# One number and one branch for each pair of experts, with the even split last in the code

## What is computed

```python
gates = jnp.sum(jax.nn.one_hot(flat_idx, N_EXPERTS, dtype=jnp.float32)
                * (g_w * e_w)[..., None], axis=1)
y = jnp.zeros((b * s, d), jnp.float32)
for e in range(N_EXPERTS):
    hid = jax.nn.silu(xt @ w_gate[e]) * (xt @ w_up[e])
    y = y + gates[:, e:e + 1] * (hid @ w_down[e]).astype(jnp.float32)
```

## Time and profile before

| | |
|---|---|
| median of three runs | 1491.67 us (1491.1 to 1496.73) |
| the profiled execution | 1496.81 us, span 1494.9 us |
| PE busy | 1265.8 us, 85% of the span |
| PEld, DVE, ACT, POOL busy | 755.1, 393.0, 286.0, 73.6 us |
| mean granted clock of TensorE | 0.917 |
| expert stages, first to last L639 | 255 to 521 us and 767 to 1028 us |

### The profile page before, as it was taken

The page is one execution under the profiler, slowest core; times in us unless marked ns, Lnnn a source line. Parts: engine busy times, 40 slices in busy tenths (PEclk is TensorE's granted clock), DMA queues, the critical chain, the costliest instruction groups (busy, mean ns, idle before and its releaser), DMA issues.

```text
span 1494.9 us, 17527 instructions
## 1 busy us (share of the span) xinstructions
PE 1265.8 (85%) x7188; PEld 755.1 (51%) x7191; DVE 393.0 (26%) x1064; ACT 286.0 (19%) x566; POOL 73.6 (5%) x126
## 2 busy tenths in 40 slices
PE   4999986779999869988768999984999877988896
PEld 1756434334444247653434343431877756756672
DVE  0213324111111025821341111112133665312122
ACT  2213311001011021142211010101103444221101
POOL 3000001000000030000000000000001221000000
PEclk9799996989999989998778999997999989998898
DMA  9976960779999969852529999999244423242000
GB/s 343 326 288 251 347 246 3 279 291 394 396 393 393 393 220 339 306 184 99 182 89 330 369 392 393 396 395 338 67 159 127 131 75 126 69 167 67 0 14 28
DMA packets 159080, 351.49 MB, mean 235 GB/s; under 512 B 4853, under 2 KB 7069, under 8 KB 159005
## 3 DMA queue, kind: packets, MB, share of 16 engines
q1 hardware_dynamic: 152776, 340.94, 62.7%
q0 software_dynamic: 4704, 6.50, 1.8%
q10 hardware_dynamic: 1524, 2.95, 0.6%
HBM read 349.25 MB, written 1.12 MB: 234 GB/s over the span
## 4 chain that ended last, share of the span: by engine, by line
PE 79%; DVE 6%; issue 5%; ACT 5%; DMA 3%; SPq 1%; DVEq 0%; ACTq 0%
PE bank L399 24%; PE bank L639 22%; PE bank L409 10%; PE bank L622 4%; PE bank L664 4%; PE bank L431 3%; DMA ring<-in_w_ada 2%; PE bank L443 2%; DMA ring<-in_moe_w_up 1%; PE bank L879 1%; PE bank L452 1%; PE bank L463 1%; ACT arena L939 1%; SPq L321 1%; PE bank L557 1%
## 5 line engine op out<-in xcount | busy, mean ns | idle before, releaser
L639 PE MATMUL bank<-ring,arena 128*32 128x512 f32 x3072 | 342.7, 602 | 40.6 <-issue 31.5
L399 PE MATMUL bank<-arena,ring 128*128 128x256 f32 x1600 | 363.3, 390 | 6.2 <-DVE arena L1295 2.8
L399 PEld LDWEIGHTS bank<-arena,ring 128*128 128x128 f32 x1600 | 313.0, 196 | 58.4 <-issue 5.6
L639 PEld LDWEIGHTS bank<-ring,arena 128*32 128x32 f32 x3072 | 112.2, 111 | 258.9 <-issue 258.9
L409 PE MATMUL bank<-ring,arena 128*128 128x512 f32 x352 | 157.8, 608 | 2.4 <-issue 2.4
L409 PEld LDWEIGHTS bank<-ring,arena 128*128 128x128 f32 x352 | 68.0, 195 | 89.4 <-issue 88.5
L622 PE MATMUL bank<-arena 128*128 128x128 f32 x512 | 70.3, 302 | 20.9 <-issue 20.9
L622 PEld LDWEIGHTS bank<-arena 128*128 128x128 f32 x512 | 67.8, 216 | 33.6 <-issue 32.8
L431 PE MATMUL bank<-ring,c_rep 128*32 128x512 f32 x480 | 68.4, 701 | 12.2 <-DMA ring<-in_w_ada 6.4
L1643 DVE TENSOR_TENSOR arena<-arena,bank 128x512 f32<-128x512 f32 x16 | 11.0, 688 | 228.2 <-PE bank L639 228.2
L980 ACT ACTIVATE arena<-bank 128x512 f32<-128x512 f32 x41 | 24.5, 596 | 238.4 <-PE bank L399 185.2
(11 more groups left out here) (267 smaller groups left out, 980.6 us busy)
## 6 DMA issues: line engine op xcount, KB each, us to landing
ring<-in_moe_w_gate SPq DMA_DIRECT2D x32, 2048.0 KB, 14.3
ring<-in_moe_w_up SPq DMA_DIRECT2D x32, 2048.0 KB, 18.5
ring<-in_moe_w_down SPq DMA_DIRECT2D x32, 2048.0 KB, 12.9
ring<-in_w_ada SPq DMA_DIRECT2D x24, 2048.0 KB, 12.9
ring<-in_w_in SPq DMA_DIRECT2D x16, 2048.0 KB, 9.2
ring<-in_w_c SPq DMA_DIRECT2D x6, 2048.0 KB, 10.0
ring<-in_ev_w_in SPq DMA_DIRECT2D x5, 2048.0 KB, 20.1
ring<-in_od_w_in SPq DMA_DIRECT2D x5, 2048.0 KB, 7.9
```

Of the source, the lines that this page charges most:

```text
L399: mm = pe.matmul(ps[k0][:, t * S:(t + 1) * S], w[:, k, c:c + P], rhs[:, k, :], start=(k == 0), stop=(k == KT - 1))
L639: mm = pe.matmul(bank[col:col + CHUNK, :], lhs[:, k, col:col + CHUNK], ring[:, s0 + e, cut], start=start, stop=stop, tile_position=(0, col))
```

## The change

`split` holds one number a pair instead of three flags. TensorE reads it once and tests it once around the whole work of the pair: `first_pair`, `middle_pair` and `last_pair` each stand three times, for n = 1, 3 and 2 in this order. What was outside the tests (gather, scatter, the turned blocks, the waits) is inside now. VectorE's rule prefers n = 2: 1 only if the first expert has up to 32 tokens and the second over 64, 3 if the first has over 64, else 2. The rows that the experts get follow from it. TensorE's wait for `late_ready` stands behind the last pair. The other lines of `gate_up` and `down` are the same, one level further out.

```diff
-        split = sb("split", [P, LAYERS, CHUNKS - 1, PAIRS], I32)
+        split = sb("split", [P, LAYERS, PAIRS], I32)
...
-                def by_split(splits, emit):
-
-                    for n in range(1, CHUNKS):
-                        with pe.If(splits[n - 1] > 0):
+                def by_split(which, emit):
+
+                    for n in (1, 3, 2):
+                        with pe.If(which == n):
                             emit(n)
...
-                def gate_up(j, splits):
+                def gate_up(j, n):
 
                     pe.wait_ge(sem("x_cur_act"), j + (done + 1))
                     pe.wait_ge(sem("x_cur_dve"), j + (done + 1))
                     if not isinstance(j, int) or j:
                         pe.wait_ge(sem("g_cur_ready"), j + done)
-                    def products(n):
-                        for bank, m0 in ((4, 0), (5, 2)):
...
-                    by_split(splits, products)
+                    for bank, m0 in ((4, 0), (5, 2)):
...
-                def down(j, splits, last=False):
+                def down(j, n, last=False):
...
-                    def products(n):
-                        for half in range(2):
...
-                    by_split(splits, products)
-
-                def splits_of(j):
+                    for half in range(2):
...
+                def split_of(j):
                     col = slice(j, j + 1) if isinstance(j, int) else bass.ds(j, 1)
-                    return [pe.value_load(split[0:1, layer, n, col], min_val=0, max_val=1) for n in range(3)]
+                    return pe.value_load(split[0:1, layer, col], min_val=1, max_val=3)
+
+                def first_pair(n):
+                    gate_up(0, n)
+                    gather(1)
+                    down(0, n)
+
+                def last_pair(n):
+                    gate_up(PAIRS - 1, n)
+                    results(PAIRS - 2)
+                    scatter(PAIRS - 2)
+                    down(PAIRS - 1, n, last=True)
+                    results(PAIRS - 1)
+                    scatter(PAIRS - 1)
 
                 gather(0)
+                by_split(split_of(0), first_pair)
+                with pe.Fori(1, PAIRS - 1) as j:
+
+                    def middle_pair(n):
+                        gate_up(j, n)
+                        results(j - 1)
+                        gather(j + 1)
+                        scatter(j - 1)
+                        down(j, n)
+
+                    by_split(split_of(j), middle_pair)
+                by_split(split_of(PAIRS - 1), last_pair)
                 pe.wait_ge(sem("late_ready"), layer + 1)
-                splits = splits_of(0)
-                gate_up(0, splits)
-                gather(1)
-                down(0, splits)
-                with pe.Fori(1, PAIRS - 1) as j:
-                    splits = splits_of(j)
-                    gate_up(j, splits)
-                    results(j - 1)
-                    gather(j + 1)
-                    scatter(j - 1)
-                    down(j, splits)
...
-                for c in range(2):
-                    step(dve.tensor_scalar(other[:, :, c], number_of[:, :, 0], float(CHUNK * (c + 1)), None, ALU.is_le))
-                step.wait()
-                step(dve.tensor_copy(split[:, layer, 0, :], other[:, :, 0]))
...
+                step(dve.tensor_scalar(few, number_of[:, :, 0], float(CHUNK), None, ALU.is_le))
+                step(dve.tensor_scalar(other_many, number_of[:, :, 1], 2.0 * CHUNK, None, ALU.is_gt))
+                step(dve.tensor_scalar(many, number_of[:, :, 0], 2.0 * CHUNK, None, ALU.is_gt))
+                step.wait()
+                step(dve.tensor_tensor(few, few, other_many, ALU.mult))
+                step.wait()
+                step(dve.tensor_tensor(lean, many, few, ALU.subtract))
+                step.wait()
+                step(dve.tensor_scalar(split[:, layer, :], lean, 2.0, None, ALU.add))
```

More of the change, by code:

```diff
@@ L648, in gate_up @@
                         pe.wait_ge(sem("g_cur_ready"), j + done)
-                    def products(n):
-                        for bank, m0 in ((4, 0), (5, 2)):
[L651 to L656, removed]
-                    by_split(splits, products)
+                    for bank, m0 in ((4, 0), (5, 2)):
+                        landed(m0, j)
+                        landed(m0 + 1, j)
+                        for k in range(KT):
+                            mm = chunks(ps[bank], x_cur, k, m0, slice(k * 512, k * 512 + 512), n,
+                                        k == 0, k == KT - 1)
+                        mm.then_inc(unit_done, 2)
                 def scatter(j):
@@ L722, in experts @@
[L722 to L728, removed]
+                    for half in range(2):
+                        for f in range(4):
+                            mm = chunks(ps[6 + half], hidT, f, 4,
+                                        slice(f * D + half * 512, f * D + half * 512 + 512), n,
+                                        f == 0, f == 3)
+                        if half == 0:
+                            mm.then_inc(sem("down_full"), 1)
+                        else:
+                            mm.then_inc(unit_done, 2)
@@ L1553, in route @@
                 mask_of = rt[:, 512:544].rearrange("p (t j a) -> p t j a", t=TT, a=2)
[L1554 removed]
                 slots = rt[:, 636:652].rearrange("p (j a) -> p j a", a=2)
[L1556 removed]
+                number = rt[:, 652:668]
                 dve.wait_ge(sem("rank_full"), layer + 1)
@@ L1562, in route @@
                 number_of = number.rearrange("p (j a) -> p j a", a=2)
-                for c in range(2):
-                    step(dve.tensor_scalar(other[:, :, c], number_of[:, :, 0], float(CHUNK * (c + 1)), None, ALU.is_le))
+                few, many, other_many, lean = (rt[:, 708 + 8 * n:716 + 8 * n] for n in range(4))
+                step(dve.tensor_scalar(few, number_of[:, :, 0], float(CHUNK), None, ALU.is_le))
+                step(dve.tensor_scalar(other_many, number_of[:, :, 1], 2.0 * CHUNK, None, ALU.is_gt))
+                step(dve.tensor_scalar(many, number_of[:, :, 0], 2.0 * CHUNK, None, ALU.is_gt))
                 step.wait()
-                step(dve.tensor_copy(split[:, layer, 0, :], other[:, :, 0]))
-                step(dve.tensor_tensor(rt[:, 708:716], other[:, :, 1], other[:, :, 0], ALU.subtract))
-                step(dve.tensor_scalar(rt[:, 716:724], other[:, :, 1], -1.0, 1.0, ALU.mult, ALU.add))
-                step(dve.tensor_tensor(n_other, other[:, :, 0], other[:, :, 1], ALU.add))
+                step(dve.tensor_tensor(few, few, other_many, ALU.mult))
                 step.wait()
-                step(dve.tensor_copy(split[:, layer, 1:3, :], rt[:, 708:724].rearrange("p (n j) -> p n j", j=PAIRS)))
+                step(dve.tensor_tensor(lean, many, few, ALU.subtract))
                 step.wait()
-                step(dve.tensor_scalar(slots[:, :, 0], n_other, -float(CHUNK), 3.0 * CHUNK, ALU.mult, ALU.add))
-                step(dve.tensor_scalar(slots[:, :, 1], n_other, float(CHUNK), float(CHUNK), ALU.mult, ALU.add))
+                step(dve.tensor_scalar(split[:, layer, :], lean, 2.0, None, ALU.add))
+                step(dve.tensor_scalar(slots[:, :, 0], lean, float(CHUNK), 2.0 * CHUNK, ALU.mult, ALU.add))
+                step(dve.tensor_scalar(slots[:, :, 1], lean, -float(CHUNK), 2.0 * CHUNK, ALU.mult, ALU.add))
                 step.wait()
```

1 line of the change is left out of this document (removed).

## The result

The changed kernel takes 1505.78 us, median of 4 runs (1505.07 to 1511.62), against 1491.38 us for the kernel before in 4 runs of the same session. The ratio is 1.0101 with a 95% interval of 1.0063 to 1.0139: slower by 1.0%. The forecast was 1494 us in a range of 1480 to 1516, with "same" slightly ahead of "slower". By the prediction's own line of 7.5 us this is "slower", which had 0.38, and not "same", which had 0.45. The time lies in the range, but outside the forecast case's own range of 1484 to 1501: it is inside only because the range was drawn wide enough for rival A's 1512. That much is luck, so the steps need a look. The ratios in this text leave out two runs far above their fellows, one of before (1787.64 us) and one of the kernel with only the new rule (4811.25 us).

A forecast was written before the change was run, and what follows sets the result against it. Weight transfers and TensorE's waits for its own code were taken to bound the expert stages. Layer 0's -6.6 and layer 1's +8.7 us sum to +2.1 on the median of 1491.67: 1494 us, range 1480 to 1516.

The forecast's parts named there:

- forecast case: The prediction's main account, both layers' changes summed to 1494 us; 1484 to 1501 by itself, chance 0.45.
- rival A: Code fetches strictly in turn: a second jump right behind another costs 3.5 us more under load; 1512 us, chance 0.22.
- What bounds the kernel: Expert stages: weight transfers take 31.9 us a pair against TensorE's 30.9, and waits for TensorE's own code.
- The jumps of the new code: Skipped bodies of nearly two blocks: far jumps once per layer, 6.2 us, 7.2 behind another; idle 3.2 and 4.2.
- step (1): Layer 0, first pair: split is read earlier, two idle jumps of 3.2 and 4.2; gate and up start 3.0 us late.
- Step (2): Layer 0, first pair: the 9.20 us gap goes; down starts 19.5 us later and ends at 284.8 against 292.2.
- step (4): Layer 0, second pair: no jump in its body, 4.17 us gone twice; down ends at 326.6 against 334.2.
- step (5): Layer 0 transfers: they run steadily from earlier, so the last "up" weights land 5.5 us earlier, at 492.3.
- Step (6): Layer 0, last pair: first jump hits, second costs 7.2 us; gate starts at 488.6, up at 495.6 against 502.2.
- Layer 1: Second expert stage: four jumps in a row behind the first pair and a lowered clock, +8.7 us in all.
- Rival B: Jumps at the tests are cheap, 3.2 us each with no extra for a second one; 1466 us, chance 0.15.
- Rival C: The loop's eight blocks aren't kept, so each pass pays three jumps of 6.2 us; +175, 1667 us, chance 0.08.

## Why the prediction was near, and what was off

**What bounds the kernel: right.** The passes follow at 31.92 to 31.93 us behind the "up" transfers, against 31.9 worked out from the queue's rate, from the fifth pair of layer 0 on. The 16 us that two reads and some tests fewer were worth did not show; that the reads bring nothing was tested by itself.

**The jumps of the new code: right in place and kind.** Every one of the ten slow tests stands where the count of instructions had put it, and the first test in front of the last pair hits (329 ns). The prices were 3.34 and 4.65 (3.2 and 4.2 forecast), 6.24 and 7.47 (6.2 and 7.2). The gaps: 12.56 for 12.3, 23.92 for 23.3, 6.53 for 6.1.

**Layer 0, steps (1) to (6), -6.6 forecast, +2.0 measured: wrong, and in two terms.** The first is step (1)'s place of the read. The first test began 3.3 us behind the gather's start (246.9 against 243.59), not 1.9; with the dearer idle jumps that makes 2.0 us. The forecast had the first products start 3.0 us later against the gather than before, and they started 5.3 later (11.7 against 6.4), outside the "2 to 4" of its own list of signs. The second and larger is the clock behind a gap. Step (2) and step (4) took 13.94 us for the products of gate and up; they took 15.73 and 15.87. The windows of the changed kernel around them and one undisturbed product between them (length, busy us, PEclk, DMA share, GB/s):

```profile
255.30:271.10 15.80, 15.80 (x129) 0.88 0.34 110
296.00:311.90 15.90, 15.90 (x129) 0.88 0.54 186
327.10:341.00 13.90, 13.90 (x132) 1.00 1.03 394
490.80:506.60 15.80, 15.78 (x129) 0.88 0.95 359
```

A mean of 0.88 says that the products behind the gaps of 7.15, 12.56 and 6.53 us ran partly at 1.2 GHz; it costs them 1.8 to 1.9 us each. The prediction had charged that in one place, layer 1's long gap, and left it out behind the four others that it forecast itself, three of them in layer 0. It gave as its condition a gap of over 20 us, but its own rows show slow products behind shorter ones: the 15.64 of the earlier trace rows stands behind 3.76, and in the earlier trace rows 112 matmuls took 14.85 behind 3.63, where 112 at the full clock take 12.2. With 2.0, 1.8 and 1.9 the steady transfers begin 5.7 us later than step (5) had it, which is all of the 5.5 that it promised: its "up" weights 5.5 us earlier did not come. SyncE's line L356 in the changed kernel, 470 to 476, the answer to the earlier trace rows:

```profile
L356 SPq DMA_DIRECT2D ring<-in_moe_w_up x2: 3103/4133/5163, 468.8 to 472.1; - x2
...
DMA to landing us min/median/max: 17.6/19.2/20.9
```

Issued at 472.1, the last "up" weights land 20.9 later at 493.0, 249.4 us behind the first gather; before it was 497.8 less 248.8, 249.0. Step (6) misses the clock twice: the "up" product of the loop's last pass, behind its wait of 2.43 us, took 8.77 instead of 7.07, and the last pair's gate and up 15.73 again, 3.5 us together. In all 9.2 us, where the layer was off by 8.6.

**Layer 1, +8.7 forecast, +11.0 measured: right, a little small.** From the first product to the last down product 262.8 us were forecast and 265.4 came, 2.6 more. The last pair's gate began 1.2 late (244.7 us behind the first product against 243.5); the pass before it had lost 1.7 to the clock (978.52, 8.77 us instead of 7.07). The same clock behind the last gap is 1.9 more (15.87 instead of 13.94), and the way from there to the down product was 0.5 shorter than forecast.

**What the clock did in the whole kernel** is less than the products' row says. They took 7.3 us more than before (342.7 to 350.0), but the gathers and scatters took less. Their rows, before and after:

```profile
L622 PE MATMUL bank<-arena 128*128 128x128 f32 x512 | 70.3, 302 | 20.9 <-issue 20.9
L664 PE MATMUL bank<-arena 128*128 128x512 f32 x128 | 60.9, 620 | 6.8 <-issue 5.0 <-DVE arena L1651 1.8
...
L622 PE MATMUL bank<-arena 128*128 128x128 f32 x512 | 63.2, 283 | 0.0
L661 PE MATMUL bank<-arena 128*128 128x512 f32 x128 | 57.9, 595 | 1.8 <-DVE arena L1651 1.8
```

The three groups together took 473.9 us before and 471.1 after. Before, the jumps stood between products and gather, and the gather ran slowly behind them (5.13 us); now they stand in front of the products. So the clock isn't a new cost of the change. It is a term that the forecast booked on one side only: step (2) took the gather's gain (3.84 for 5.13) and not what the products would lose. Nor is the length of the gap the whole of it. The products of gate and up took 13.94 us behind 1.51 in the kernel without tests, in the one with the even split first and in layer 1 of the changed kernel. But they were slow behind 2.10 in layer 1 of before:

```profile
837.07 15.64 PE L639 MATMUL bank<-ring,arena 128*32 128x512 f32 x128 [2.10 <-issue]
```

They were slow too behind 1.64, with another gap of 2.2 shortly before it, in the kernel with only the new rule (126 matmuls in 16.78 us) and in the one with the tests around the products (123 in 15.36). No run held the gaps and changed the clock alone, so it isn't shown which gaps bring it down.

**Rival A, fetches strictly in turn: wrong.** A second miss right behind another costs 1.2 to 1.3 us more, not 3.5 (7471 and 7568 ns against 6242 and 6244). Its packets overlap: in layer 0 the two of the second miss began 0.3 us apart (291.14 and 291.46) and took 1.4 and 2.1 us, where the one of the first miss took 1.1. 1512 was nearer to the time than 1494, for another reason than the rival gave.

**Rival B, cheap jumps: wrong under load, right when idle.** 6.2 against 3.3 us for the same kind of jump.

**Rival C, the loop isn't kept: wrong by one block.** It was given 0.08 and 1667 us; one body more brings 1773. (Its sum should give 1654: three jumps of 6.2 less 2.7 are 15.9, not 17.) The prediction said that no run showed the fit, and so it was: nothing in the trace of before showed more than seven blocks.

**What the prediction did not ask** is which part of the change does what. The sum mixed the rule's gain with the bodies' cost. Taken apart: the rule -0.9%, the number nothing, the bodies around the whole pair with the even split last +2.0% (1505.78 against 1476.72).

## What to carry to other kernels

Code that a branch skips isn't free: count the instructions of a skipped body in blocks of 256, and keep it short, or write it once in a loop that is entered once. A loop with its skipped bodies has to fit in eight blocks; the ninth costs more than anything that a test saves. Where a step is expected to leave TensorE idle, add the slow clock behind it (here 1.8 to 1.9 us behind each of the gaps of 6.5 to 24 us) at every place, not only at the longest, and look at what ran slowly there before.

## What the runs showed of the hardware

- A failed test whose target was not yet asked for took 3.3 to 3.8 us with the transfers idle and 6.2 us with them running; a second one right behind it 4.6 to 4.8 and 7.3 to 7.6 us.
- What running transfers add to such a test is nearly all time before the packet with the code starts. In the changed kernel it started 0.9 us behind the test with the transfers idle (247.8 against 246.9), and 3.7 and 3.8 us behind it with them running (285.3 against 281.6, 792.0 against 788.2); the packet itself took 0.9 and 1.1 us.
- A loop of eight blocks of 256 instructions, by the prediction's count, ran without a fetch; one of nine fetched nine blocks in a pass, one of ten fetched ten. The step from one to the other, one body that is never run, cost 267 us, 247 of them in the 12 passes.
- Waits of 2.4 us for a transfer lowered the clock in some passes (8.77 us for the "up" product) and not in others (7.07), behind waits of the same length (2.43 and 2.44).
